# Cached keys in units of eight whole pages instead of half the features of sixteen, and the first unit's scores five steps earlier in the prompt's items

## What is computed

```python
def forget_attn_sample(q, k_new, v_new, c_new, k_past, v_past, c_past):
    cq = c_new.transpose(0, 2, 1)[..., None]
    s_past = jnp.einsum('nqhd,nkhd->nhqk', q, k_past).astype(jnp.float32) * ATTN_SCALE
    s_past = s_past + cq - c_past.transpose(0, 2, 1)[:, :, None, :]
    ...
    p = jax.nn.softmax(jnp.concatenate([s_past, s_new], axis=-1), axis=-1)
    out = jnp.einsum('nhqk,nkhd->nqhd', p[..., :past].astype(v_past.dtype), v_past)
    return out + jnp.einsum('nhqk,nkhd->nqhd', p[..., past:].astype(v_new.dtype), v_new)
```

## Time and profile before

| | us |
|---|---|
| median of 3 runs | 1410.33 |
| lowest, highest | 1407.0, 1413.3 |
| the profiled execution | 1410.16 |
| its span, first to last instruction | 1408.1 |
| PE busy in the span | 1292.0 (92%) |
| DVE, ACT, POOL busy | 513.0, 309.1, 168.8 |
| mean granted TensorE clock | 0.94 |

### The profile page before, as it was taken

How to read it: one execution, slowest core, us unless ns; L and a number is a source line. 1 busy time by engine, 2 the same in 40 slices (tenths; PEclk the granted TensorE clock), 3 DMA queues, 4 the chain that set the end, 5 groups by cost and what they waited for, 6 DMA issues and landing times.

```text
span 1408.1 us, 36243 instructions
## 1 busy us (share of the span) xinstructions
PE 1292.0 (92%) x15268; PEld 976.8 (69%) x15268; DVE 513.0 (36%) x1323; ACT 309.1 (22%) x767; POOL 168.8 (12%) x202
## 2 busy tenths in 40 slices
PE   6979999999897999999989799979998799999996
PEld 5869999998545767667665455545446799999983
DVE  3740000000275636464655556664026200000005
ACT  2201111111141131414145353535011011111110
POOL 3110000010202111121211111211000100000003
PEclk9969999999988999999999787989998799999999
DMA  8959999998998799899988797976273599999986
GB/s 280 384 179 364 387 389 391 389 391 336 335 361 277 229 319 344 293 345 306 347 275 291 261 314 243 332 235 227 109 283 142 204 375 385 391 390 390 390 320 209
DMA packets 147222, 437.00 MB, mean 310 GB/s; under 512 B 20711, under 2 KB 51304, under 8 KB 138270
## 3 DMA queue, kind: packets, MB, share of 16 engines
q1 hardware_dynamic: 99494, 367.58, 70.6%
q10 hardware_dynamic: 37296, 38.09, 8.3%
q0 software_dynamic: 10320, 29.79, 6.7%
HBM read 406.32 MB, written 29.44 MB: 309 GB/s over the span
## 4 chain that ended last, share of the span: by engine, by line
PE 64%; issue 12%; DMA 7%; DVE 6%; SPq 4%; ACT 4%; ACTq 1%; POOL 1%; DVEq 0%; POOLq 0%
PE PS L1102 12%; PE PS L1106 11%; PE PS L1355 9%; PE PS L1134 6%; PE PS L1139 6%; PE PS L1492 5%; PE PS L1024 3%; DMA W<-in_cache_v 3%; PE PS L1395 3%; SPq L684 2%; PE PS L1433 2%; PE PS L1456 2%; DMA KV<-in_cache_k 1%; PE PS L1117 1%; PE PS L1442 1%
## 5 line engine op out<-in xcount | busy, mean ns | idle before, releaser
L1106 PE MATMUL PS<-W,KV 128*32 128x128 f32 x3072 | 345.5, 275 | 0.0
L1102 PE MATMUL PS<-W,KV 128*32 128x384 f32 x3072 | 342.2, 491 | 3.2 <-DVE KV L2054 3.2
L1106 PEld LDWEIGHTS PS<-W,KV 128*32 128x32 f32 x3072 | 337.7, 111 | 2.2
L2294 DVE TENSOR_TENSOR KV<-KV,PS 128x384 f32<-128x384 f32 x32 | 17.7, 554 | 482.8 <-PE PS L1120 426.7
L1355 PE MATMUL PS<-W 128*128 128x256 f32 x768 | 177.6, 385 | 0.7 <-ACT KV L1764 0.7
L1355 PEld LDWEIGHTS PS<-W 128*128 128x128 f32 x768 | 143.9, 192 | 31.4 <-issue 11.1
L1134 PE MATMUL PS<-W,KV 128*32 128x384 f32 x1440 | 162.2, 488 | 0.0
L1139 PE MATMUL PS<-W,KV 128*32 128x256 f32 x960 | 162.2, 327 | 0.0
L2433 DVE STREAM_TRANSPOSE KV<-KV 128x1024 f32<-128x1024 f32 x128 | 155.5, 1230 | 8.1 <-DMA KV<-in_cache_k 8.0
L1102 PEld LDWEIGHTS PS<-W,KV 128*32 128x32 f32 x3072 | 150.8, 110 | 4.5 <-DVE KV L2054 4.1
L1139 PEld LDWEIGHTS PS<-W,KV 128*32 128x32 f32 x960 | 95.6, 109 | 14.4
(11 more groups left out here) (305 smaller groups left out, 1449.8 us busy)
## 6 DMA issues: line engine op xcount, KB each, us to landing
W<-in_w_gate SPq DMA_DIRECT2D x32, 2048.0 KB, 14.5
W<-in_w_up SPq DMA_DIRECT2D x32, 2048.0 KB, 15.7
W<-in_w_down SPq DMA_DIRECT2D x32, 2048.0 KB
KV<-in_cache_k SPq DMA_DIRECT2D x256, 256.0 KB, 5.4
W<-in_cache_v SPq DMA_DIRECT2D x128, 512.0 KB, 8.2
yd<-KV ACTq DMA_DIRECT2D x30, 288.0 KB, 8.0
W<-in_w_kvf SPq DMA_DIRECT2D x4, 2048.0 KB, 18.2
W<-in_w_kvf ACTq DMA_DIRECT2D x8, 1024.0 KB, 7.8
```

The lines of the kernel that those rows point to most:

```text
L1102: pe.matmul(PS[32 * q:32 * q + 32, bank, 0:WIDE], x, w[:, k, 0:WIDE], start=(k == 0), stop=(k == KC - 1), tile_position=(0, 32 * q), skip_ ...
L1106: mm = pe.matmul(PS[CAP:P, bank, P * q:P * q + P], x, w[:, k, WIDE:FF], start=(k == 0 and q == 0), stop=(k == KC - 1), tile_position=(0, C ...
```

## The change

Three things are changed.

1. A key unit is now eight whole pages, all 1024 features. Each page is one DMA of 128 rows of 4 KB, 8 DMAs for a unit in place of 16. The four parts of the scores remain; a part is now 64 matmuls with 256 columns in place of 32 with 512. The first unit's parts fill the left half of each PSUM bank, the second's the right half. DVE's transposes keep their number (8 for each unit), size and steps.
2. `PromptTicks.QK` is (1, 3, 14, 16) in place of (6, 8, 14, 16).
3. The first unit of item 0 is loaded in pairs of pages at the same four values of `summed`.

```diff
--- before.py
+++ after.py
@@ -114,7 +114,7 @@
     V = (6, GROUPS + 2)
-    QK = (6, 8, 14, 16)
+    QK = (1, 3, 14, 16)
     MID = 2
@@ -463,7 +463,7 @@
-        KU = [a.rearrange("p a (g n) -> p (a g) n", n=HALF) for a in (KB, VB)]
+        KU = [a.rearrange("p a (g n) -> p (a g) n", n=D) for a in (KB, VB)]
@@ -680,9 +680,9 @@
             def load_keys(i, h, ch):
-                for g, page in enumerate(page_numbers(i, ch)):
-                    sp.dma_start(KU[h][:, CH * ch + g, :], k_rows[bass.ds(page * PAGE, PAGE), HALF * h:HALF * h + HALF])\
-                        .then_inc(sem(f"k_in{h}_{ch // 2}"), 16)
+                for g, page in enumerate(page_numbers(i, 2 * h + ch)):
+                    sp.dma_start(KU[h][:, CH * ch + g, :], k_rows[bass.ds(page * PAGE, PAGE), :])\
+                        .then_inc(sem(f"k_in{h}_{ch}"), 16)
@@ -695,9 +695,10 @@
-            for ch in (1, 2, 3, 0):
-                sp.wait_ge(sem("summed"), ch + 1 if ch else NT)
-                load_keys(0, 0, ch)
+            for ch, half, last in ((0, 1, 2), (1, 0, NT - 2), (1, 1, NT - 1), (0, 0, NT)):
+                sp.wait_ge(sem("summed"), last)
+                for g, page in list(enumerate(page_numbers(0, ch)))[2 * half:2 * half + 2]:
+                    sp.dma_start(KU[0][:, CH * ch + g, :], k_rows[bass.ds(page * PAGE, PAGE), :]).then_inc(sem(f"k_in0_{ch}"), 16)
@@ -707,7 +708,7 @@
-            for ch in range(4):
+            for ch in range(2):
                 load_keys(0, 1, ch)
@@ -1484,14 +1485,16 @@
-                    for e in range(2):
-                        for a in range(4):
-                            lo = 2 * (4 * s2 + a) + e
-                            for x in range(4):
-                                rows = slice(32 * x, 32 * x + 32)
-                                mm = pe.matmul(PS[32 * a:32 * a + 32, x, :], QB32[rows, 16 * h + lo, :], KU[h][rows, :, 32 * lo:32 * lo + 32],
-                                               start=(part == 0 and e == 0), stop=(part == 3 and e == 1),
-                                               tile_position=(32 * x, 32 * a), skip_group_check=True)
+                    keys = 2 * P
+                    for s4 in (2 * s2, 2 * s2 + 1):
+                        for e in range(2):
+                            for a in range(4):
+                                lo = 2 * (4 * s4 + a) + e
+                                for x in range(4):
+                                    rows = slice(32 * x, 32 * x + 32)
+                                    mm = pe.matmul(PS[32 * a:32 * a + 32, x, keys * h:keys * h + keys], QB32[rows, lo, :],
+                                                   KU[h][rows, :, 32 * lo:32 * lo + 32], start=(s4 == 0 and e == 0), stop=(s4 == 3 and e == 1),
+                                                   tile_position=(32 * x, 32 * a), skip_group_check=True)
@@ -2427,9 +2430,9 @@
             def keys_transposed(i, h, x):
-                if x % 4 == 0:
-                    dve.wait_ge(sem(f"k_in{h}_{x // 4}"), 128 * (i + 1))
-                pages = KU[h][:, 2 * x:2 * x + 2, :].rearrange("p g n -> p (g n)")
+                if x % CH == 0:
+                    dve.wait_ge(sem(f"k_in{h}_{x // CH}"), 64 * (i + 1))
+                pages = KU[h][:, x, :]
```

## The result

The changed kernel is slower: 1434.33 us (median of 4 runs, 1432.1 to 1437.6) against 1411.82 us for the kernel before on the same chip, a ratio of 1.016 with a 95% interval of 1.012 to 1.020. The forecast was 1406 us, with a range of 1394 to 1422: the kernel is 28 us slower than forecast, and 12 us slower than the upper end. The profiled execution took 1433.37 us; its span is 1431.6 us, 23.5 us over the span before.

A forecast was written before the change was run, and what follows sets the result against it. The prediction took PE's work and standing time to bound the kernel in attention. Its terms, from +11.2 for the key parts to -11.4 us for value waits, summed to -4.0: 1410.2 - 4.0 = 1406.2, so 1406 us, range 1394 to 1422.

The forecast's parts named there:

- Term 1: All 32 key parts: 64 smaller matmuls add pauses on PE, 0.35 us a part, +11.2 us.
- Term 2: Steps 6 and 8 of items 4 to 7: waits for ACT's copy get uncovered, 1.0 us an item, +4 us.
- Rival B: Steps 6 to 8 and after, items 4 to 7: uncovered waits bring the slow clock, 1421 us; chance 0.20.
- Term 3: First round of item 4: PE's wait for DVE's scaling goes, -2.4 us, and slow-clock time comes back, -2 us.
- Term 4: Step 2 of items 5 and 7: both waits for values go, -11.4 us; slow clock around them, -0.7 us.
- Term 5: Start of item 0: DVE's wait for the first key unit shrinks, -2 us; the second unit's wait, -0.7 us.
- The term that was set to 0: Items 0 to 3: SP issues saved later are on nobody's path, 0 us.

The follow-up runs named there:

- E1: Kernel before with only the split, each key part as 64 matmuls of 256 columns, own loads and steps: 1442.23 us, ratio 1.020.
- E7: Changed kernel with 40 PE semaphore updates once ahead of item 4, shifting later PE instructions by 40 places: 1446.54 us, ratio 1.024.
- E6: Changed kernel with key loads of items 5 to 7 cut to 16 of each page's 128 rows: 1434.03 us, ratio 1.017.
- E2: Kernel before with only the first unit's key parts of items 4 to 7 moved to steps 1 and 3: 1386.81 and 1391.51 us.
- E3: Changed kernel with key parts back at steps 6 and 8, so whole-page units alone: 1443.16 us, ratio 1.023.
- E9: Kernel before with value loads of items 4 to 7 cut to 16 of each page's 128 rows: 1407.52 us, ratio 0.996.
- E4: Changed kernel with one more wait on SP, holding back item 1's bias loads and what SP issues behind them: 1429.66 us, ratio 1.012.
- E5: Kernel before with both the split and steps 1 and 3, but its own loads: 1433.13 us, ratio 1.015.

## Why the prediction was wrong

**Term 1 (+11.2 us) had the right mechanism and missed the larger half of the price.** A part went from 2.28 to 2.69 us, 0.41 and not 0.35: 13.1 us for 32 parts. The weight loads do come in four lots, as the prediction had it, with 0.65 us from lot to lot. In items 4 to 7 the line's busy time rose by 13.6 us (39.4 to 53.0) for 16 parts, since four of them now run at the lower clock (4.0 to 4.4 us, at 810.88, 879.44, 944.31 and 975.41) where one did. And the step that failed is "64 matmuls are four lots of sixteen, with three pauses in place of one", as if that were all that more records cost. A part is now 128 matmuls and 128 loads, 256 instructions, and one 16-KB packet holds 256 of them (the 2048 records more, at two instructions each, came with 16 packets more). PE eats a packet in 2.69 us where it took some 4.6 before, and two parts with one step between eat two. Then it stands: 13.4 us of gaps in the changed kernel, up to 3.5 us each. E1 shows that they come with the split, E7 that they sit at fixed places of the program, the counts between gaps that these are the ends of packets, E6 that they hardly depend on the load traffic, and the queue shows a packet of q8 in the gap itself, from 843.0 to 844.4:

```profile
q8 instruction: 1, 0.02, 5.2%
```

The Trainium skill has the numbers behind this: "Advanced Engine Details and Errata" (ISA Cache) gives a line of 16 KB with 256 instructions. The trace agrees: 16 packets for 4096 instructions, and 254 to 256 counted ones between neighbouring gaps. "Runtime: NRT & Kernel Launch" (Instruction fetch mechanics) says that the fetch runs ahead by itself and that its cost is mostly hidden, as the sequencer issues more slowly than the fetch fills. Here the trace disagrees, with 13.4 us in the changed kernel and 19.5 in E1.

**Term 2 (+4 us) held.** L1434 waits 7.2 us for ACT's copy (5.7 before), the line behind it 9.4 us (6.8 before): 4.1 us more. At step 8 it is 0.57 us instead of 1.0, for instance in item 5:

```profile
827.25 1.09 PE L1434 MATMUL PS<-W 65*128 65x144 f32 x6 [0.57 <-ACT W L1931]
```

Rival B, the clock falling after these waits, is not what made the kernel slow: the clock of items 4 to 7 rose, from 0.87 to 0.91.

**Term 3 (-2.4 and -2 us) held in its wait**: item 4 starts with the key parts, and no wait stands ahead of L1445. Two gaps of 1.26 and 0.51 us have come there in its place, and the value matmuls at step 10 now run at the lower clock (3.62 us at 763.13, 1.89 before), so of the -2 us for the clock little is left.

**Term 4 (-11.4 us) held, and its clock (-0.7) was right where it looked and missed the rest.** Both waits are gone. At step 2 the lower clock stayed, as the prediction read it from item 5's end: it moved to the key part (4.40 us at 810.88). But the value line fell by 11.6 us in E2 and by 7.1 in the changed kernel (42.9 to 35.8). What step 2 gave of that the key parts took back; the rest came from step 27, of which the prediction has no row: its four groups took 3.5 to 3.6 us before and take 1.93 now. That the waits caused this is not shown. E3 has no waits for values and a value line of 40.6 us; E9 has 8.6 us of them and 36.9 us.

**Term 5 (-2 and -0.7 us)**: DVE's 7.46 us became 5.81, -1.6; the 1.09 us stayed 1.08, so the -0.7 did not come.

**The term that was set to 0** cost 10 us: "the SP issues saved later in items 0 to 3 are on nobody's path". Those of item 0 were on the path of a store. I had named the place ("if the stores and weight loads of ACT's queue got less of the DMA engines from them, PE would wait"), but gave it no price and no rival. Its row would have been SP's: bias behind sixteen key issues at 504.08, a store at 501.69. Halving the issues puts the bias ahead of the store. E4 shows that what SP issues there is the cause, and not which of its loads.

Added up by rows: start -1.7; key parts +7.3 and +13.6; gaps +13.4; the wait in item 0 +9.9; values' waits and clock -11.4 and -7.1; item 4's wait -2.4; uncovered waits +4.1; behind attention +2.1. That is +27.8, and the spans differ by 23.5; the other 4.3 us lie in smaller groups, which were not taken apart. Against the forecast the two large misses are the gaps (13.4 us) and the wait in item 0 (9.9 us); the key parts cost 20.9 us instead of 11.2. What step 27 gave was luck, since no term counted on it.

**What stays open** is the clock. The split takes 13.1 us by its parts and 13 by its gaps, 26 us, but costs 42 to 46 when the steps are moved. The missing part is PE busy longer on other lines (239.1 us in E5 against 215.4 in E2, of which the key parts are 10.7). The gaps may bring the lower clock: in the changed kernel the three value groups that run at it (763.13, 850.19 and 983.44) each stand within 5 us behind a gap. But no run here takes the gaps away and leaves the split. And why the moved steps alone raise the clock at step 27 is as open.

## What to carry to other kernels

When the same columns are cut into more, smaller matmuls, count the instructions as well as the columns: a burst that uses up 256 of them in under 3 us can leave PE standing for its own program, and the page's row of the instruction queue shows the growth. An edit that saves DMA issues moves everything behind them on that queue; write down what is issued next, and which other queue's transfer it will now overtake. Before you put the lower clock down to a wait, look at where it begins: here it began ahead of the wait for values, and after the reorder it fell on the work that had moved there. And try the parts of a change by themselves: the moved steps alone beat both kernels, by 22 to 27 us over the kernel before, of which the waits are 11.4.

## What the hardware showed that I had not expected

- PE standing for instructions while its inputs are ready: gaps of up to 3.8 us at ends of 256-instruction packets, with 2.60 us left of 3.47 when the DMA engines were busy 0.43 instead of 0.96.
- A semaphore update of PE's queue as an instruction of its own is not cheap: with 128 of them a key part took 18.2 us instead of 2.3, some 120 ns each.
- A 128-KB store that was done 8.4 us after its issue took 18.2 us when four bias loads were issued 2.6 us ahead of it instead of 2.4 us behind; with SP's loads held back it took 8.9 us again.
- The steps of two key parts alone moved the granted clock of a 240-us stretch from 0.86 and 0.87 (three profiles) to 0.92 and 0.93 (two).
